# Each low part of a weight unit computed in two GpSimd operations of 512 columns instead of one of 1024

## What is computed

```
h    = rmsnorm(x);  parts = h @ w_in                    # layer 1: q, k, v, mLSTM parts, gates
att  = sliding_window_attention(...);  hm = mlstm_chunkwise(...)
x    = x + (sigmoid(ga) * (att @ Wa) + sigmoid(gm) * (hm @ Wm)) @ w_out
x    = x + peer_ffn(rmsnorm(x))     # per token and head: top 16 of 16384 experts, rows gathered
xn   = rms_norm(x);  parts = xn @ w_in_2                # layer 2
o_sb = stick_breaking_attention(...);  o_hg = hgrn2_mixer(...)
h    = x + (sigmoid(g1) * (o_sb @ B1) + sigmoid(g2) * (o_hg @ B2)) @ w_out_2
out  = h + (silu(hn @ w_gate) * (hn @ w_up)) @ w_down,  hn = rms_norm(h)
```

## Time and profile before

| what | value |
|---|---|
| three runs | 1373.81, 1375.44, 1378.73 us; median 1375.44 |
| the profiled execution | 1373.92 us, its span 1372.20 us, mean granted TensorE clock 0.956 |
| busy in the span | TensorE 1200.6 us (87%), VectorE 716.9 (52%), ScalarE 576.9 (42%), GpSimd 831.4 (61%) |
| GpSimd's low parts, L429 | 206 of 1024 columns, 498.9 us busy, 2439 ns mean |
| DMA | 381.86 MB; 420 GB/s in the picks stage |

### The profile page before, as it was taken

How to read it: one execution, slowest core, us unless ns; L and a number is a source line. 1 busy time by engine, 2 the same in 40 slices (tenths; PEclk the granted TensorE clock), 3 DMA queues, 4 the chain that set the end, 5 groups by cost and what they waited for, 6 DMA issues and landing times.

```text
span 1372.2 us, 16858 instructions
## 1 busy us (share of the span) xinstructions
PE 1200.6 (87%) x6468; PEld 872.5 (64%) x6468; DVE 716.9 (52%) x1453; ACT 576.9 (42%) x1264; POOL 831.4 (61%) x509
## 2 busy tenths in 40 slices
PE   6899999995998778788877877787999999999998
PEld 6797899993433333233333333333999899999997
DVE  4735217257967585766758576555487413211111
ACT  6365656452423232224323232225566365544442
POOL 6656658955664545454454555441876458788885
PEclk9899999997999999999899999999999999999999
DMA  8423445629999999999999999998544335455551
GB/s 249 154 93 102 145 126 191 210 66 412 426 425 425 425 426 425 426 426 425 426 425 427 425 426 427 425 427 301 184 159 142 100 123 184 151 188 184 184 186 60
DMA packets 138417, 381.86 MB, mean 278 GB/s; under 512 B 8545, under 2 KB 99681, under 8 KB 105569
## 3 DMA queue, kind: packets, MB, share of 16 engines
q0 software_dynamic: 36864, 268.45, 46.6%
q1 hardware_dynamic: 100000, 112.25, 25.2%
q10 hardware_dynamic: 1472, 0.09, 0.1%
HBM read 379.72 MB, written 1.05 MB: 277 GB/s over the span
## 4 chain that ended last, share of the span: by engine, by line
PE 50%; DMA 30%; DVE 11%; ACT 6%; issue 2%; POOL 1%; ACTq 0%; DVEq 0%; SPq 0%
PE ps L645 30%; DMA rows_w<-peer_rows_in,arena 29%; PE ps L864 9%; PE ps L1031 4%; DVE rows_w L1890 2%; PE ps L983 2%; ACT w_hi L421 1%; DVE arena L1890 1%; DMA ring<-w_in_in 1%; ACT arena L1150 1%; ACT wgt L1314 1%; PE ps L938 1%; POOL rows_w L605 1%; PE ps L728 1%; DVE arena L1615 0%
## 5 line engine op out<-in xcount | busy, mean ns | idle before, releaser
L429 POOL TENSOR_TENSOR w_lo<-ring,w_hi 128x1024 fp32r<-128x1024 f32 x206 | 498.9, 2439 | 222.0 <-ACT w_hi L421 221.9
L864 PE MATMUL ps<-arena,diag 128*128 128x512 f32 x448 | 231.2, 668 | 86.9 <-ACT diag L1320 86.9
L864 PE MATMUL ps<-rows_w,diag 128*128 128x512 f32 x512 | 240.2, 613 | 32.6 <-ACT diag L1320 32.6
L421 ACT ACTIVATE w_hi<-ring 128x1024 fp32r<-128x1024 f32 x206 | 211.7, 1057 | 134.4 <-PE ps L645 96.2
L645 PE MATMUL ps<-hT_hi,w_hi 128*128 128x256 f32 x816 | 235.4, 288 | 7.9 <-POOL w_lo L429 7.9
L605 POOL DMA_INDIRECT arena<-peer_rows_in,arena x112 | 130.7, 1167 | 182.2 <-PE ps L864 165.0
L864 PEld LDWEIGHTS ps<-arena,diag 128*128 128x128 f32 x448 | 90.9, 211 | 224.0 <-ACT diag L1320 122.9
L645 PE MATMUL ps<-hT_lo,w_hi 128*128 128x256 f32 x816 | 232.6, 285 | 0.0
L645 PE MATMUL ps<-hT_hi,w_lo 128*128 128x256 f32 x816 | 232.4, 285 | 0.0
L605 POOL DMA_INDIRECT rows_w<-peer_rows_in,arena x128 | 165.6, 1294 | 104.1 <-PE ps L864 90.5
L1890 DVE CUSTOM_DVE_ANT_0 rows_w<-rows_w,arena 128x1024 f32<-128x1024 f32 x128 | 156.4, 1225 | 115.6 <-DMA rows_w<-peer_rows_in,arena 115.4
(11 more groups left out here) (382 smaller groups left out, 1720.1 us busy)
## 6 DMA issues: line engine op xcount, KB each, us to landing
ring<-w_in_in SPq DMA_DIRECT2D x45, 1024.0 KB, 5.1
ring<-w_ffn_gate_in SPq DMA_DIRECT2D x11, 1024.0 KB, 5.1
ring<-w_ffn_up_in SPq DMA_DIRECT2D x11, 1024.0 KB, 5.2
ring<-w_ffn_down_in SPq DMA_DIRECT2D x11, 1024.0 KB, 5.1
ring<-w_out_in SPq DMA_DIRECT2D x8, 1024.0 KB, 5.0
ring<-w_branch_attn_in SPq DMA_DIRECT2D x4, 1024.0 KB, 5.2
ring<-w_branch_mlstm_in SPq DMA_DIRECT2D x4, 1024.0 KB, 4.9
ring<-peer_w_query_in SPq DMA_DIRECT2D x4, 1024.0 KB, 4.9
```

What stands on the lines that cost most here:

```text
L421: act.activation(hi_of(n, u)[:, t, 0:cols], raw_half(n, g)[:, t, 0:cols], ACT.Copy).then_inc(sem("hi_ready"), 1)
L429: pool.tensor_tensor(lo_of(n, u)[:, t, 0:cols], raw_half(n, g)[:, t, 0:cols], hi_of(n, u)[:, t, 0:cols].bitcast(F32), ALU.subtract).then_i ...
L864: ins = pe.matmul(acc[:, c, :], diag[:, p % 4, :], pick_row(p % TOPK, D + c * CW, CW), start=False, stop=True, skip_group_check=True)
```

## The change

A unit's subtraction is issued as two operations, on the first and on the second two of its four blocks of 256 columns (512 columns each; 544 in the first half). `lo_ready` rises once for each unit, as before, now with the second operation.

```
             for u, t, cols in split_units(n, g):
                 pool.wait_ge(sem("hi_ready"), u + 1)
-                pool.tensor_tensor(lo_of(n, u)[:, t, 0:cols], raw_half(n, g)[:, t, 0:cols], hi_of(n, u)[:, t, 0:cols].bitcast(F32),
-                                   ALU.subtract).then_inc(sem("lo_ready"), 1)
-
-
-
+                for p in (slice(t.start, t.start + KU // 2), slice(t.start + KU // 2, t.stop)):
+                    ins = pool.tensor_tensor(lo_of(n, u)[:, p, 0:cols], raw_half(n, g)[:, p, 0:cols], hi_of(n, u)[:, p, 0:cols].bitcast(F32), ALU.subtract)
+                ins.then_inc(sem("lo_ready"), 1)
```

## The result

The changed kernel takes 1378.89 us (median of 22 runs, 1375.93 to 1383.87), the kernel before beside it 1375.4 (22 runs). The ratio is 1.002, 95% interval 1.0011 to 1.0029: +2.75 us, between +1.5 and +4.0. The profiled execution has a span of 1376.8 us (before 1372.2).

A forecast was written before the change was run, and what follows sets the result against it. DMA bounds the picks stage, TensorE the stages before and behind; GpSimd is no bound but holds VectorE up. Five places sum 0.2 - 0.2 + 0.25 + 1.1 + 0.25 = +1.6 us on 1375.44: 1377.0, range 1370.5 to 1382.5.

The forecast's parts named there:

- the case that I held likeliest: VectorE and GpSimd take turns, fixed cost between 0.05 and 0.25: 1374 to 1380 us, chance 0.62.
- place 4: 1053 to 1073 us, behind the picks: L2009, which frees L902, ends later, +1.1 us (0 to +3.5).
- Fixed cost: Each unit's additional GpSimd operation costs 0.15 us; 208 units add 31 us, hidden where TensorE is the bound.
- Its sum of +3.1: Total over the kernel with the skill's 0.31 us for an operation's fixed cost, instead of +1.6 us.
- slower rival: At 1053 to 1073 us the late collision costs two halves: +4.5 us in all, 1380; chance 0.17.
- a: Fixed cost of one GpSimd operation on a low part, taken as 0.15 us.
- Turns: Where VectorE meets GpSimd's units, one operation goes through for each piece; two halves can hold two operations, 1.2 us won for one.
- faster rival: At all five places each VectorE wait is halved and nothing takes the other half: -14 us, 1361; chance 0.12.
- Places 1 to 3: Before the picks: 25 to 58 us +0.2, 93 to 116 us -0.2, 297 to 306 us +0.25.
- +0.25 for the first gather: 297 to 306 us: the same end behind 2 x 0.15 more of GpSimd, going through the picks to the end.
- Feed-forward loop: A unit of 2.55 us stays under TensorE's 2.73, so GpSimd's added time is hidden there.
- place 5: At 1183 us L2092's two operations wait one for each of the last unit's halves: +0.25 us.

The follow-up runs named there:

- e1: Kernel before with only the units of the first stage (before the picks) made in two operations; ratio 0.9991, -1.2 us.
- e5: Changed kernel with ten units (four at 985 to 996 us, six at 1053 to 1076 us) in one operation again; 0.9991 against the kernel before, -1.2 us.
- e10: Kernel before with one more VectorE operation, an in-place multiplication by 1.0, in front of the first L2009; ratio 1.0018, +2.5 us.
- e8: Kernel before with four operations for units of the first stage and from 1046 us up to the feed-forward loop; ratio 0.9940, -8.2 us.
- e2: Kernel before with only the units between the picks stage and the feed-forward loop made in two operations; ratio 1.0034, +4.7 us.
- e3: Kernel before with only the feed-forward units made in two operations; ratio 1.0003, +0.4 us.
- e9: Kernel before with only the first stage's units made in eight operations of 128 columns; ratio 1.0083, +11.4 us.
- e7: Kernel before with only the first stage's units made in four operations of 256 columns; ratio 0.9949, -7.0 us, 1366.7 us.

## Why the prediction was right, and where it was not

Forecast +1.6 us, 1377.0; measured +2.75, 1378.9: within the range, in the case that I held likeliest. But the sum came out through terms that partly cancel, and two terms with the clock in them were not in it at all: the mechanism of place 4 was right, that the total came so near was in part luck.

- *Fixed cost.* 0.15 predicted, 0.14 measured, busy time +31 predicted, +36 measured (the rest are halves that VectorE held up). Quarters and eighths have the same: 2.78 and 3.36 us a unit are 2.36 + 3 x 0.14 and 2.36 + 7 x 0.14. The 0.31 worked out from the Trainium skill (GPSIMD Engine Reference, "3.1 Elementwise — side-by-side cycle accounting") was twice too much. Its sum of +3.1 lies nearer to the measured time than mine, but not for its reason; the prediction shows no steps for it, and its own slower rival has +4.5 for every a from 0.2 on.
- *Turns.* One operation, one piece: seen at L1613 (four in 4.31 to 4.34 us), at L1832 and L1835, at L1985 and L1986. In front of the first gather the halves held L1834 and L1837, not L1832 and L1833 as predicted. The gates chain gained 0.16 us, and L725's wait grew by 0.24. The kernel before breaks the rule once, which the prediction passed over (last section). The faster rival's -14 us fell with this.
- *Places 1 to 3.* I had +0.25 for the first gather. Of the profiles with TensorE's slow start, five with the first stage halved reach it at 306.05 on average (305.26 to 306.59), three with it whole at 307.01 (306.78 to 307.39): a gain of about 1 us. Counted from VectorE's first L1600 in all ten it is 275.90 against 277.02 us. e1 says the same in time (-1.2), with 0 at the edge of its interval; e5's -1.2 does not, since its profile gains behind the picks stage. Sign wrong, size small. What the gain comes from is not shown: the wait of L680 for ScalarE fell from 2.3 to 1.6 us, but those for L1691 grew from 1.7 to 2.9 (3.2 in e10, whose units are whole), and in e10 the stretch from L725 to the last L680 is as short as in e1 (100.95 and 100.93 us).
- *Place 4.* +1.1 predicted by L2009's later end, and the mechanism was the predicted one: L938's wait went (0.2), ScalarE handed over its unit earlier, L1986 met the half that starts just before it. VectorE, 1070 to 1075 us, as the earlier trace rows:

```profile
1071.44 0.68 DVE L1985 TENSOR_TENSOR arena<-arena 128x512 f32<-128x512 f32 x1
1072.04 1.75 DVE L1986 TENSOR_TENSOR arena<-arena 128x512 f32<-128x512 f32 x1
1073.72 0.94 DVE L2007 TENSOR_TENSOR arena<-arena,ps 128x768 f32<-128x768 f32 x1
```

  and GpSimd beside it, as the earlier trace rows:

```profile
1054.54 13.64 POOL L430 TENSOR_TENSOR w_lo<-ring,w_hi 128x512 fp32r<-128x512 f32 x8 [2.46 <-ACT w_hi L421]
1071.79 4.37 POOL L430 TENSOR_TENSOR w_lo<-ring,w_hi 128x512 fp32r<-128x512 f32 x3 [3.61 <-ACT w_hi L421]
```

  The wait cost +1.07, but the step "L2009, which frees L902, ends 1.1 us later: +1.1" had nothing for TensorE's clock behind a longer wait. Windows of the changed kernel (busy, clock):

```profile
1070.00:1075.00 5.00, 0.41 (x3) 0.76 0.56 193
1075.00:1080.00 5.00, 5.00 (x19) 0.55 0.23 76
...
1365.00:1370.00 5.00, 3.79 (x10) 0.66 0.00 0
```

  and of the kernel before:

```profile
1070.00:1075.00 5.00, 2.34 (x5) 0.73 0.07 26
1075.00:1080.00 5.00, 5.00 (x39) 0.93 0.49 157
...
1365.00:1370.00 5.00, 3.97 (x18) 1.00 0.42 157
```

  The stretch grew by 1.7 to 2.0 us in all four profiles with this wait, and in none of the others. The kernel before loses clock here too, behind its 2.7 us: from the end of the wait to L983 it is 53.5 us in the three profiles whose clock stays at 1.00 (e5, e8, e10), 55.0 and 55.1 in the two of the kernel before and 55.7 to 55.9 in the four. So the missing term is 0.8 us, on top of 1.5 that the kernel before pays.
- *A place that I missed.* I looked only at where VectorE waits for GpSimd, and not at where GpSimd waits for VectorE: 0.55 us idle at 996 us, in the changed kernel's two profiles and in e2.
- *The end.* 1.5 to 1.6 us in the last 24 matmuls. The wait in front of them is 2.14 or 2.15 us in every profile, and the halves don't touch them (e3: 5.35). The lower clock came in five profiles, which reach L1015 at 1357.64 or between 1364.42 and 1366.39, and not in the nine others, at 1352.48, 1354.57, 1374.65 and from 1361.23 to 1364.00. So in these fourteen it goes with when the stretch comes, here because of the 3 us before it. That is a pattern, not a test: why those moments, no run tells.
- *Feed-forward loop and place 5*: nothing and +0.1, as reasoned (+0.25).

By the runs with one stage halved, the predicted sum had +0.25 where about -1 was (e1), and +1.35 where +4.7 was (e2), in the level stage.

## What to carry to other kernels

When two engines take turns at something that they both need, count pieces: a run of m operations waits for about min(m, pieces queued) pieces, so cutting the other engine's work in two can cost as much as it saves, and the next cut can pay; work the sum out for several sizes, and at both engines. Cut only in the stage where a chain waits, and keep the pieces' fixed costs under the cover that the bounding engine gives. A wait of TensorE that grows costs more than its length if the clock falls behind it, so put that into the sum as a term of its own, from rows at both levels.

## What I had not expected of the hardware

An operation doesn't always get its turn. In e9, VectorE, 115 to 131 us:

```profile
118.11 11.51 DVE L1682 TENSOR_TENSOR am<-am 128x4 f32<-128x4 f32 x1 [2.25 <-ACT am L1151]
```

A VectorE operation on four columns ran 11.51 us, while 28 pieces of GpSimd's run of 32 (116.98 to 131.40) ended, and TensorE's L680 waited 4.8 us for what follows from it. In e7 one at 22.26 us ran 7.07 us, to the end of GpSimd's run:

```profile
22.26 7.15 DVE L1585 TENSOR_TENSOR gt<-arena,ifbias 128x16 f32<-128x16 f32 x2 [5.08 <-ACT arena L1091]
```

Whole units do it too, and the kernel before already had it. A cast that takes 0.17 us at 305.39 ran through both units that GpSimd made from 315.73 to 320.40:

```profile
315.26 5.18 DVE L1843 CAST arena<-arena 128x16 uint32<-128x16 f32 x1
```

It did so in all five profiles whose units are whole there (5.17 or 5.18 us) and in the five with halves (5.44, behind four halves); TensorE did not wait for it. The Trainium skill (SBUF — State Buffer, "Who interferes with whom") says that whoever issues first has the shared pair for the whole instruction; most waits here end so, at the next piece's end, but these did not, and no run shows what sets them apart. Small pieces are not the condition, as the cast shows, but the longest hold, 11.51 us, stood in a run of 32 of the smallest pieces, and that is a reason of its own against eighths.

The other surprise is TensorE's start: 18 or 19 matmuls between 17 and 19 us in two profiles of the kernel before and in e7, 10 to 14 in the eleven others, of which six had a granted clock of 1.00 in the same window. It moves the first stage by up to 3 us, and a single pair of profiles puts that on the wrong account.
